# Who multiplies the state-space input weights by the norm's factors: GpSimd in place of ScalarE

## The reference, cut to what matters

```
x = _layernorm(DEEPNORM_ALPHA * x + ffn, ln2_g[l], ln2_b[l])   # end of block one
...
h = rms_norm(x, mix_norm[layer])        # x / rms(x) * gain, gain has 1024 entries
# in s5_mixer:
u = (h @ w_in).reshape(bsz, seq, SSM_GROUPS, SSM_GROUP)        # w_in is 1024 x 1024
```

## Time and profile before

| | us |
|---|---|
| median of 3 executions | 1690.87 |
| lowest and highest | 1690.79, 1691.12 |
| the profiled execution, its own time | 1690.65 |
| span of its trace | 1688.8 |
| TensorE busy | 1671.8 |
| VectorE busy | 971.8 |
| ScalarE busy | 716.8 |
| GpSimd busy | 713.4 |

### The profile page before, as it was taken

The page is one execution under the profiler, slowest core; times in us unless marked ns, Lnnn a source line. Parts: engine busy times, 40 slices in busy tenths (PEclk is TensorE's granted clock), DMA queues, the critical chain, the costliest instruction groups (busy, mean ns, idle before and its releaser), DMA issues.

```text
span 1688.8 us, 22701 instructions
## 1 busy us (share of the span) xinstructions
PE 1671.8 (99%) x8664; PEld 1378.6 (82%) x8664; DVE 971.8 (58%) x1682; ACT 716.8 (42%) x1219; POOL 713.4 (42%) x336
## 2 busy tenths in 40 slices
PE   9999999999999999999999999999999999999999
PEld 7887888888888788789888888889766888888887
DVE  4777899677966759433451351558774326217235
ACT  3433254244244755434332342476864333333332
POOL 4433202403303132534485485554721254844845
PEclk9999999999999999999999999999999999999999
DMA  9522235454545468314413414132201251342331
GB/s 254 102 76 86 64 117 161 125 152 125 169 123 159 131 229 291 100 62 125 142 46 113 149 40 148 38 100 73 76 1 38 75 162 62 88 149 63 93 125 56
DMA packets 241898, 189.61 MB, mean 112 GB/s; under 512 B 40576, under 2 KB 198912, under 8 KB 241792
## 3 DMA queue, kind: packets, MB, share of 16 engines
q1 hardware_dynamic: 239920, 182.79, 35.8%
q10 hardware_dynamic: 1872, 5.37, 0.9%
HBM read 168.73 MB, written 19.40 MB: 111 GB/s over the span
## 4 chain that ended last, share of the span: by engine, by line
PE 87%; DVE 7%; ACT 2%; issue 2%; POOL 1%; DMA 0%; DVEq 0%; ACTq 0%; POOLq 0%
PE ps L422 15%; PE ps L423 14%; PE ps L424 14%; PE ps L450 6%; PE ps L452 6%; PE ps L451 6%; PE ps L667 4%; PE ps L670 4%; PE ps L669 4%; PE ps L544 1%; PE ps L545 1%; PE ps L546 1%; PE ps L1106 1%; PE ps L1136 1%; DVE x_rows L2137 1%
## 5 line engine op out<-in xcount | busy, mean ns | idle before, releaser
L1333 POOL TENSOR_TENSOR w_lo<-w_raw,w_hi 128x1024 fp32r<-128x1024 f32 (+2 forms) x220 | 533.4, 2440 | 873.6 <-ACT w_hi L1514 831.0
L422 PE MATMUL ps<-a_hi,w_hi 128*128 128x512 f32 (+1 forms) x1184 | 442.1, 373 | 0.0
L423 PE MATMUL ps<-a_lo,w_hi 128*128 128x512 f32 (+1 forms) x1184 | 440.4, 372 | 0.0
L424 PE MATMUL ps<-a_hi,w_lo 128*128 128x512 f32 (+1 forms) x1184 | 440.4, 372 | 0.0
L1514 ACT ACTIVATE w_hi<-w_raw 128x1024 fp32r<-128x1024 f32 (+3 forms) x259 | 259.4, 1022 | 124.7 <-DMA w_raw<-in_ffn_w_gate_up_dram 42.9
L422 PEld LDWEIGHTS ps<-a_hi,w_hi 128*128 128x128 f32 x1184 | 223.0, 188 | 40.4 <-issue 1.9
L424 PEld LDWEIGHTS ps<-a_hi,w_lo 128*128 128x128 f32 x1184 | 223.0, 188 | 38.5
L423 PEld LDWEIGHTS ps<-a_lo,w_hi 128*128 128x128 f32 x1184 | 223.1, 188 | 38.3
L2709 DVE TENSOR_TENSOR ev<-ps,xh 128x512 f32<-128x512 f32 x44 | 30.4, 691 | 294.2 <-PE ps L424 250.3
L1333 POOL TENSOR_TENSOR side_lo<-side_raw,w_hi 128x1024 fp32r<-128x1024 f32 (+1 forms) x60 | 132.0, 2234 | 27.5 <-ACT w_hi L1514 27.5
L2651 DVE TENSOR_TENSOR x_rows<-x_rows,ps 128x512 f32<-128x512 f32 x96 | 64.2, 686 | 105.0 <-PE ps L670 104.7
(11 more groups left out here) (393 smaller groups left out, 2792.3 us busy)
## 6 DMA issues: line engine op xcount, KB each, us to landing
w_raw<-in_ffn_w_gate_up_dram SPq DMA_DIRECT2D x88, 512.0 KB, 3.8
w_raw<-in_w_up_dram SPq DMA_DIRECT2D x44, 512.0 KB, 4.0
w_raw<-in_w_in_dram SPq DMA_DIRECT2D x20, 512.0 KB, 4.6
w_raw<-in_w_down_dram SPq DMA_DIRECT2D x20, 512.0 KB, 3.8
side_raw<-in_ffn_w_down_dram SPq DMA_DIRECT2D x20, 512.0 KB, 5.7
w_raw<-in_ffn_w_down_dram SPq DMA_DIRECT2D x20, 512.0 KB, 3.3
s_records<-stage SPq DMA_DIRECT2D x16, 544.0 KB, 5.3
w_raw<-in_ssm_w_glu_dram SPq DMA_DIRECT2D x16, 512.0 KB, 4.6
```

The lines of the kernel that those rows point to most:

```text
L422: pe.matmul(bank, wh, xh_, start=first, stop=False)
L423: pe.matmul(bank, wh, xl_, start=False, stop=False)
L424: return pe.matmul(bank, wl, xh_, start=False, stop=last)
L1333: pool.tensor_tensor(lo, raw, w_hi[:, n % RING, 0:w].bitcast(F), ALU.subtract).then_inc(lo_made, 1)
```

## The change

The multiplication of U0 to U7 by the factors goes from ScalarE to GpSimd. ScalarE had two operations a chunk (one for each half, with the factor as the operation's scale). GpSimd has one for the chunk, a product of two tensors in which the factors are repeated along the columns. ScalarE waits for a new semaphore, `gained`, before it makes the high part. Chunks of other products that have factors stay as they were.

```
+        pool_gains = range(chunks_at["u"], chunks_at["u"] + 2 * TT)
...
+            def apply_gain(n):
+
+                _, kn, cn, gain = chunk_src[n]
+                pool.wait_ge(*landed(n))
+                w = w_raw[:, n % RING, 0:kn * cn].rearrange("p (k c) -> p k c", k=kn)
+                pool.tensor_tensor(w, w, gain.unsqueeze(2).to_broadcast([P, kn, cn]), ALU.mult).then_inc(gained, 1)
+
+            gains_done = [0]
+
+            def gains_ahead(n):
+
+                while gains_done[0] < len(pool_gains) and pool_gains[gains_done[0]] <= n + 1:
+                    apply_gain(pool_gains[gains_done[0]])
+                    gains_done[0] += 1
+
             for n, (_, kn, cn, _) in enumerate(chunk_src):
+                gains_ahead(n)
                 if n in vector_chunks:
                     continue
...
-                    if gain is not None:
+                    if n in pool_gains:
+                        act.wait_ge(gained, pool_gains.index(n) + 1)
+                    elif gain is not None:
                         for k in range(kn):
```

More of the change, by code:

```diff
@@ L249, in program @@
         w_used = sem("w_used")
+        gained = sem("gained")
         side_landed = [sem(f"side_landed{i}") for i in range(4)]
```

## The result

| | us |
|---|---|
| before, median of 14 executions | 1690.91 (1690.71 to 1691.35) |
| after, median of 14 executions | 1694.86 (1692.68 to 1696.68) |
| ratio | 1.0022, 95% interval 1.0015 to 1.0028 |
| profiled execution after: its time, its span | 1694.87, 1693.0 |

The changed kernel is 4.0 us slower, and its times scatter over 4 us where those of before lie within 0.6. Both want an explanation.

A forecast was written before the change was run, and what follows sets the result against it. TensorE, busy 1671.8 of 1688.8 us, was taken as the bound, so only its waits count. Two stalls, 3.62 + 0.91 = 4.5 us, on 1690.65 gave 1695.2, with 0.22 for the median 1695.4 us; range 1692.8 to 1698.6.

The forecast's parts named there:

- the clock: Rival: TensorE's clock falls to 1.2 GHz after the wait before U2, up to 3.9 us more, 1699.3 us; chance 0.05.
- The exclusion and its turns: VectorE operations with two SBUF tensors and GpSimd operations don't run together; they alternate, the one already waiting going next.
- the walk: Turn-by-turn end times of GpSimd and VectorE operations from U2's product to tile 3's transposes, at 591.25 instead of 587.63.
- The first stall: Around U2 and tile 3's layernorm, turns on VectorE and GpSimd make TensorE's transposes of tile 3 3.62 us later.
- The second stall: U7's product behind U6's and U5's low part delays ScalarE's copies, so L949 starts 0.91 us later.
- elsewhere ScalarE waited anyway: Away from U2 and U3, relieving ScalarE gains nothing: it waited 6.36, 2.14 and 1.40 us for chunks to land.
- The length of a product: One GpSimd product with the norm's factors takes 1.90 us, taken from L1282, with 2.39 as upper bound.
- the rival with 2.39: Each GpSimd product takes as long as a low part, 2.39 us: 7.7 us in all, 1698.6 us; chance 0.12.
- The estimate of 2.2 us: GpSimd product length from the skill's 2.6 cycles an element at 1.2 GHz; six products add 1.9 us, 1697.3 us.
- The lost race: Rival: U4 lands after 584.3, so U2's low part runs first; first loss 2.0, sum 2.9, 1693.8 us; chance 0.18.

The follow-up runs named there:

- idle products: Against the kernel before: ScalarE multiplies all eight chunks as before, GpSimd also runs eight products on a scratch buffer nobody reads; 1695.28 us, ratio 1.0024.
- the two kernels that move U4's turn: The change, with GpSimd's product of U4 also waiting for VectorE's low part of U2 (1691.73 us), or for L2158 of tile 3 (1692.79 us).
- U0, U1, U6 and U7: The change with only these four chunks multiplied on GpSimd, U2 to U5 on ScalarE; 1693.84 us, ratio 1.0017.
- U0, U6 and U7: The change with only these three chunks multiplied on GpSimd, the others on ScalarE; 1691.60 us, ratio 1.0004.
- reciprocal first: The change, with the reciprocal rms(3) ahead of the two low parts in VectorE's stream; 1694.75 us, ratio 1.0021.
- U4 behind U2's low part: The change, with GpSimd's product of U4 also waiting until VectorE has made U2's low part; 1691.73 us, ratio 1.0005.
- U2 alone, twice: The change with only U2 multiplied on GpSimd and U1's low part ahead of it in GpSimd's stream; 1690.04 and 1690.11 us.
- U2 to U5: The change with only U2, U3, U4 and U5 multiplied on GpSimd, the others on ScalarE; 1695.22 us, ratio 1.0027.
- Two halves of the change: The change with GpSimd multiplying only U2 to U5 (1695.22 us), or only U0, U1, U6 and U7 (1693.84 us).

## Why the prediction came out right, and where its sum was off

Forecast 1695.4 us, measured 1694.86; the side and the mechanism were right. How near the number came is in part luck: of the 4.5 us of the sum, 0.9 did not come, and the clock, which the sum left out, added a few tenths to the median. The seven executions that kept the full clock and did not lose the race have a median of 1694.54, 3.6 us above before.

**The exclusion and its turns** carried the forecast and held to within 0.1 us. With 0.36 of start-up added, the walk had the product of U2 end at 578.28 (trace 578.27), L2156 at 581.76 (581.72), L2158 at 584.62 (584.55), TensorE start on U2 at 587.56 (587.53) and on the transposes at 591.61 (591.52). The idle products show that it is the operations that collide, not the waits around them. The page "SBUF — State Buffer" of the Trainium skill, section "Who interferes with whom", describes the lock on the shared ports and names VectorE's operations with two SBUF inputs; the trace agrees (1.28 us becomes 2.80, and L2064, with one operand in PSUM, keeps its 0.645). The order of turns, on which 2.2 to 3.0 us of the result depend (3.95 us for the change, 1.71 and 0.92 for the two kernels that move U4's turn, the clock's share included), came from the earlier trace rows alone.

**The first stall** was put at 3.62 us. Measured to where TensorE's stream runs without a gap again (588.26 before, 592.37 after, less 0.36) it is 3.75. The 0.13 more is an error of reading: the transposes' start before was taken from the chain (587.63), which cuts off what overlaps the matmul ahead of them; in the timeline they start at 587.47, and behind a wait nothing overlaps.

**The second stall** is the term that was mis-sized: 0.91 us forecast, zero in the profile. It exists (0.8 and 0.6 us of waiting at L950 with U0, U1, U6 and U7, and with U0, U6 and U7), but in the full change it is paid back, and the step that failed is "elsewhere ScalarE waited anyway": taking U4's product off ScalarE is worth something. ScalarE issues the loads of the first state-space records at about the time of U4's chunk work, and in the kernel before these loads still share the DMA engines with U6. The table has the issue of the first records' load, the issue of U6 and the start of the work on U6, from the timelines of ScalarE's queue, of SyncE's and of the engine that multiplies U6:

| kernel | U4 multiplied by | records issued | U6 issued | U6 started | U6's issue to start |
|---|---|---|---|---|---|
| before | ScalarE | 590.65 | 594.13 | 598.91 | 4.8 |
| U0, U6, U7 | ScalarE | 591.04 | 594.52 | 599.17 | 4.7 |
| U0, U1, U6, U7 | ScalarE | 592.67 | 596.15 | 600.97 | 4.8 |
| the change | GpSimd | 592.90 | 598.24 | 602.14 | 3.9 |
| reciprocal first | GpSimd | 591.47 | 596.81 | 600.64 | 3.8 |
| U4 behind U2's low part | GpSimd | 590.13 | 595.47 | 599.29 | 3.8 |

Where ScalarE multiplies U4 the records go out 3.5 us ahead of U6's transfer, where it doesn't 5.3 us ahead, and U6 is 0.9 us less on its way. The eight other traces agree: 4.5 to 4.7 us with U4 on ScalarE (U2 alone, twice, and the idle products), 3.7 to 4.0 without (the other five, among them U2 to U5, where ScalarE itself multiplies U6). The DMA queues show what lies between. Queue q10 carries ScalarE's loads of the records, here while U6 is on its way (594.1 to 598.9 us) in the kernel before:

```profile
q10 hardware_dynamic: 119, 0.45, 24.2%
```

and in the change (598.2 to 602.1 us):

```profile
q10 hardware_dynamic: 3, 0.00, 0.3%
```

So before, 0.45 MB of records still move beside U6's 0.5 MB, and in the change they are through. This pays for the copies: they end at 611.87, and TensorE comes to L950 at 611.99. It is read from the traces; a kernel that moves only the records' loads wasn't run.

**The length of a product** was 1.90 us as taken, so the rival with 2.39 is out. The estimate of 2.2 us from the Trainium skill's page "GPSIMD Engine Reference" (section "Elementwise — side-by-side cycle accounting") was too high for this form, with its second operand repeated; its advice against such work on GpSimd was borne out for the eight products, for another reason than speed, and not for U2's alone, which came out 0.8 us ahead.

**The lost race** was given 0.18 and 1693.8 us. Made on purpose it takes 1692.8, since its sum held the second stall too; 4 of 23 executions fall in its band.

**The clock** was given 0.05, at 1699.3 us, and this was misjudged both ways. It falls in about half of the executions, 12 of 23, but costs the median one only a few tenths: 0.96 us of it hides in the wait before tile 3's transposes, and in the profiled one it lasted 3.4 us. The earlier trace rows could not speak for a wait of 2.8 us, since the longest in the kernel before is 1.5.

**What the prediction did not see** is how close the kernel before stood to losing 2 us in another place: the low part of U1 comes 0.8 us too late to disturb tile 0's layernorm. In the change the new order in GpSimd's stream hides this by chance.

## What to carry to other kernels

Before work is moved to GpSimd, lay VectorE's timeline beside the stretch: in all these traces, operations of VectorE with two tensors in SBUF and GpSimd's products and low parts exclude one another and take turns, the one already waiting first, so that work which nobody waits for can delay the critical engine by its whole length each time. Walk the turns through in order, with the landing times, and look also at what the relieved engine now does sooner, because an operation that comes in earlier can take a turn that it used to lose. Where it must be moved, move the one operation that lies on the path and keep the others out of the stretch: here one product of eight gave 0.8 and 1.0 us (with intervals that still take in no change), and all eight cost 4.0.

## What the runs showed of the hardware that was not expected

- The granted clock fell to 0.5 (1.2 GHz) in some executions of the same program and not in others, behind a wait of 2.8 us that was the same in the two that were profiled: between 588.2 and 588.4 us in one, a microsecond after TensorE had begun to work again. Behind a wait of 4.9 us it had fallen in all five executions, in the profiled one before the wait was over.
- Two halves of the change lost more than the whole: 4.4 and 3.0 us apart, 4.0 together.
- A transfer of 512 KB was put to use 0.9 us sooner after its issue where other loads had been started 1.9 us further ahead of it, so that 0.45 MB of them no longer moved beside it.
